# An expert layer whose items are paired by size: counts sorted on chip, biases by matmul, the first expert fetched whole, results gathered by index

## The reference

```
logits = hf @ router_w + router_b
top_logit, top_idx = lax.top_k(logits, 4)
gates = jax.nn.softmax(top_logit, axis=-1)
...
def expert_block(xb, e):
    gu = xb @ w_gu[e] + b_gu[e]                 # 1024 -> 2 x 1024
    gate, up = gu[..., :1024], gu[..., 1024:]
    gate = jnp.minimum(gate, 7.0)
    up = jnp.clip(up, -7.0, 7.0)
    y = (up + 1.0) * (gate * jax.nn.sigmoid(1.702 * gate))
    return y @ w_down[e] + b_down[e]            # 1024 -> 1024
...
out = segment_sum(y_rows * row_gate)            # four rows a token
x = x + g2 * out
result = rmsnorm(x, final_g)
```

## Time and profile before

| | |
|---|---|
| median of three runs | 3612.41 us (3611.96 to 3616.03) |
| span of the profiled execution | 3608.5 us |
| TensorE busy | 86% of the span |
| VectorE / ScalarE / GpSimd busy | 40% / 25% / 8% |
| moved by DMA | 684.11 MB, mean 190 GB/s |
| mean granted TensorE clock | 0.931 |

### The profile page before, as it was taken

How to read it: one execution, slowest core, us unless ns; L and a number is a source line. 1 busy time by engine, 2 the same in 40 slices (tenths; PEclk the granted TensorE clock), 3 DMA queues, 4 the chain that set the end, 5 groups by cost and what they waited for, 6 DMA issues and landing times. The chain is left out here.

```text
span 3608.5 us, 95079 instructions
## 1 busy us (share of the span) xinstructions
PE 3112.7 (86%) x42406; PEld 2242.3 (62%) x42406; DVE 1452.6 (40%) x2335; ACT 898.5 (25%) x1523; POOL 298.1 (8%) x236
## 2 busy tenths in 40 slices
PE   5978879998887888787897976676999999999996
PEld 3855558887565676674786866543566566666653
DVE  3355653333763554556565765524111111111111
ACT  2114322222223343332343542201011000111100
POOL 0021200000411132230000104000000000000000
PEclk7989889999898999997998987887999999999998
DMA  7242432222143101003653430222999999999993
GB/s 288 82 158 77 155 140 85 101 96 93 38 155 123 50 21 38 34 4 125 233 187 121 166 115 3 101 102 94 399 404 406 408 407 405 406 405 406 409 405 139
DMA packets 220724, 684.11 MB, mean 190 GB/s; under 512 B 26096, under 2 KB 51184, under 8 KB 187712
## 3 DMA queue, kind: packets, MB, share of 16 engines
q1 hardware_dynamic: 190288, 647.72, 46.8%
q10 hardware_dynamic: 30192, 32.77, 2.7%
HBM read 659.46 MB, written 20.97 MB: 189 GB/s over the span
## 5 line engine op out<-in xcount | busy, mean ns | idle before, releaser
L3480 PE MATMUL experts_psum_gu<-ring,experts_x 128*32 128x256 f32 x9216 | 507.9, 381 | 16.6 <-ACT experts_x L3524 16.6
L3480 PEld LDWEIGHTS experts_psum_gu<-ring,experts_x 128*32 128x32 f32 x9216 | 295.6, 110 | 219.8 <-ACT experts_x L3524 16.9
L3584 DVE TENSOR_TENSOR experts_gate<-experts_psum_gu,experts_bias 128x768 f32<-128x768 f32 x32 | 30.6, 957 | 864.4 <-PE experts_psum_gu L3480 864.4
L3503 PE MATMUL experts_psum_down<-experts_weights,experts_hiddenT 128*32 128x256 f32 x6144 | 339.0, 380 | 4.3 <-ACT experts_hiddenT L3532 4.3
L3503 PEld LDWEIGHTS experts_psum_down<-experts_weights,experts_hiddenT 128*32 128x32 f32 x6144 | 199.5, 110 | 137.9 <-issue 6.3
L818 PE MATMUL mlp_psum_bank<-mlp_x_high,mlp_w_high 128*128 128x512 f32 (+1 forms) x512 | 174.8, 341 | 12.8 <-DVE xT_rounded L322 12.8
L3528 ACT ACTIVATE experts_sigmoid<-experts_gate 128x768 f32<-128x768 f32 x32 | 27.0, 843 | 615.5 <-DVE experts_gate L3586 615.5
L296 DVE TENSOR_TENSOR ring_rounded<-ring,mlp_w_high 128x1024 fp32r<-128x1024 f32 x128 | 156.7, 1225 | 51.3 <-ACT mlp_w_high L291 51.3
L818 PE MATMUL mlp_psum_bank<-xT_rounded,mlp_w_high 128*128 128x512 f32 (+1 forms) x512 | 175.4, 342 | 0.0
L818 PE MATMUL mlp_psum_bank<-mlp_x_high,ring_rounded 128*128 128x512 f32 (+1 forms) x512 | 173.6, 339 | 0.0
L3480 PE MATMUL experts_psum_gu<-xT,experts_x 128*32 128x256 f32 x3072 | 171.6, 379 | 0.0
(11 more groups left out here) (729 smaller groups left out, 5761.9 us busy)
## 6 DMA issues: line engine op xcount, KB each, us to landing
ring<-in_w_gu SPq DMA_DIRECT2D x186, 1024.0 KB, 18.9
experts_weights<-in_w_down SPq DMA_DIRECT2D x128, 1024.0 KB, 20.7
ring<-in_ada_w SPq DMA_DIRECT2D x36, 2048.0 KB, 9.0
ring<-in_mlp_w SPq DMA_DIRECT2D x32, 2048.0 KB, 7.9
xT<-in_w_gu SPq DMA_DIRECT2D x64, 1024.0 KB, 20.3
ring<-in_w_in SPq DMA_DIRECT2D x12, 2048.0 KB, 7.6
ring<-in_ab_w_in SPq DMA_DIRECT2D x6, 2048.0 KB, 9.1
ring<-in_w_rkv SPq DMA_DIRECT2D x6, 2048.0 KB, 8.4
```

The costliest lines, as they stand in the source:

```text
L3480: mm = nc.tensor.matmul(pg[o, q, gr, :], x, w[:, c:c + C], start=(u == 0 and gr != 1), stop=(u == U - 1), skip_group_check=True)
L3503: mm = nc.tensor.matmul(pd[o, gr, :], hidT[:, ch, gr, GROUP * v:GROUP * v + GROUP], w[:, ch, C * c:C * c + C], start=(v == 0 and ch == 0 a ...
L3584: v.tensor_tensor(gt[:, :, :], pg[:, 0, 0:GROUPS, :], rep(bias[:, 0, :], GROUPS), ALU.add).then_inc(s_bg, 1)
```

## The change

- The experts are ranked by their counts on chip (`ahead`: a comparison of keys, count times 32 minus the expert's number, with expert 0 put first). Items come in pairs: an item of 96 slots from the larger half (A), an item of 64 slots from the smaller half (B). The table has expert and first slot of each; a further A item stands for an expert of more than 96 tokens. The loop goes over pairs, so its body holds an A and a B item.
- Expert 0 always comes first, and its two remaining gate/up units and four down units are loaded during the router.
- The gate/up biases are split into three bf16 parts on 96 partitions (GpSimd, during the router) and added by bf16 matmuls with a 0/1 band `who` that ScalarE copies for each item; the bias loads and VectorE's two additions go.
- A down unit holds two neighbouring rows a partition, 8 KB in one run; the hidden values are transposed with stride two to match.
- The tokens are split into two rounded parts, and the gather is rounded matmuls, four for each of 16 results.
- Results are stored by item, not by slot. At the end each (token, k) row is gathered from memory by its index (GpSimd, eight indirect DMAs of 128 rows), weighted and summed on VectorE; `gsel`, its transposes and the final matmuls go. Rows of `moe_y` that a larger count would use are set to zero in the router.

The core of the diff:

```diff
 router, sync:
     sync.dma_start(w[:, :, :], rw.rearrange("(a p) n -> p a n", p=P)).then_inc(s_ld, 16)
+    for q in range(3):
+        sync.dma_start(b32[32 * q:32 * q + 32, :, :], b_gu.rearrange("e (a n) -> e a n", a=2)).then_inc(s_b32, 16)
     sync.dma_start(bd[:, :], bdown).then_inc(s_ld, 16)
+    for u in range(GU_UNITS, UNITS):
+        sync.dma_start(unit_tile(g, base, more, u), unit_rows(w_gu, w_down, 0, u)).then_inc(s_unit[u], 16)
+    sync.wait_ge(s_l, 2)
+    sync.wait_ge(s_tok, 4)
+    for u in range(2 * SLOTS, GU_UNITS):
+        sync.dma_start(unit_tile(g, base, more, u), unit_rows(w_gu, w_down, 0, u)).then_inc(s_unit[u], 16)
+    sync.wait_ge(s_zero, 1)
+    (two stores of zeros to moe_y, 960 and 640 rows)
 router, tensor:
     for t in range(2):
-        mm = nc.tensor.matmul(pb[:, n % 4, :], htok[:, t, kt * P:(kt + 1) * P],
-                              S[:, t, sh * 512:(sh + 1) * 512], start=(t == 0), stop=(t == 1))
+        for q, x in enumerate((t_high, t_low)):
+            mm = nc.tensor.matmul(pb[:, n % 4, :], x[:, t, kt * P:(kt + 1) * P],
+                                  S[:, t, sh * 512:(sh + 1) * 512], start=(t + q == 0), stop=(t + q == 2))
 router, scalar:
+    act.wait_ge(s_split, 5)
     for n in range(2 * KT):
         act.wait_ge(s_xg, n + 1)
         nc.scalar.copy(XgT[...], pb[:, n % 4, :]).then_inc(s_xgc, 1)
 router, gpsimd:
+    for q in range(3):
+        v.tensor_copy(band[r, :, :], rep(blk(g, C_ID)[r, r], GROUP, 2)).then_inc(s_pad, 1)
+    v.memset(zero[:, :], 0.0).then_inc(s_zero, 1)
+    pool.wait_ge(s_b32, 48)
+    for rows in (96, 64, 32):
+        if rows < 96:
+            v.tensor_tensor(b32[0:rows, :, :], b32[0:rows, :, :], b96_2[0:rows, :, :], ALU.subtract).then_inc(s_split, 1)
+        v.tensor_copy(b96_2[0:rows, :, :], b32[0:rows, :, :]).then_inc(s_split, 1)
 router, vector:
+    for n in range(4):
+        v.tensor_tensor(t_low[:, n // 2, cols], pb[:, n, :], t_high[:, n // 2, cols].bitcast(F32), ALU.subtract)
-    (item table in one row; gsel: 2 x (1 + 3 x 2) operations of 1024 columns)
+    (ranks, places and table by small operations on 32 partitions; the row index yidx)

 experts, tensor:
+    for gr in range(groups):
+        for q in range(2):
+            for j in range(4):
+                c = 1024 * q + C * j
+                nc.tensor.matmul(pg[32 * j:32 * j + 32, q, gr, :], who[:, :], b96[:, c:c + C],
+                                 start=(gr != 1), stop=False, skip_group_check=True)
-    with pe.Fori(0, last) as i:
-        gate_up(i + 1)
-        down(i)
-        turn_hidden(i + 1)
+    with pe.Fori(0, last) as i:
+        gate_up(i, 1)
+        down(i, 0)
+        turn_hidden(i, 1)
+        gate_up(i + 1, 0)
+        down(i, 1)
+        turn_hidden(i + 1, 0)
 experts, scalar:
-    load_bias(expert_of(act, i + 2))
+    nc.scalar.copy(who[:, :], band[:, bass.ds(e, 1), :].rearrange("p e c -> p (e c)")).then_inc(s_who, 1)
 experts, vector:
-    v.tensor_tensor(gt[:, :, :], pg[:, 0, 0:GROUPS, :], rep(bias[:, 0, :], GROUPS), ALU.add).then_inc(s_bg, 1)
-    v.tensor_scalar(gt[:, :, :], gt[:, :, :], SWI_LIMIT, None, ALU.min).then_inc(s_gt, 1)
+    v.tensor_scalar(G, pg[:, 0, 0:groups, :], SWI_LIMIT, None, ALU.min).then_inc(s_gt, 1)

 final, gpsimd:
+    for t in range(2):
+        for k in range(TOP_K):
+            n = TOP_K * t + k
+            nc.gpsimd.indirect_dma_start(out=yl[:, n, :], out_offset=None, in_=y_dram[:, :],
+                                         in_offset=bass.IndirectOffsetOnAxis(ap=yidx[:, t, k:k + 1], axis=0))\
+                .then_inc(s_yl[n], 16)
 final, tensor:
-    (16 transposes of gsel, 64 records of matmul over the 4 MB list)
 final, vector:
+    (for each tile and k: wait for the gather; total = row * gate + total)
+    ch.link(v.tensor_tensor(total[:, t, :], total[:, t, :], gate_row, ALU.mult))
+    v.tensor_tensor(g.x[:, 2 + t, :], g.x[:, 2 + t, :], total[:, t, :], ALU.add).then_inc(s_x, 1)
```

More of the change, by code:

```diff
@@ L3194, in router @@
         mask = ph.sb("mask", [P, 2, N_EXP])
-        base = ph.sb("base", [P, 2, N_EXP])
+        start = ph.sb("slot_start", [P, 2, N_EXP])
+        rank = ph.sb("slot", [P, 2, TOP_K])
         gT = ph.sb("gatesT", [N_EXP, 2, P])
[L3197 to L3203, removed]
+        cnt = ph.sb("counts", [N_EXP, P])
+        e_col = ph.sb("expert_col", [N_EXP, 2])
+        e_row = ph.sb("expert_row", [N_EXP, N_EXP])
+        key = ph.sb("keys", [N_EXP, N_EXP + 1])
+        ahead = ph.sb("ahead", [N_EXP, N_EXP])
+        vec = ph.sb("items_counts_one", [N_EXP, 4])
+        place = ph.sb("first_start_rank", [N_EXP, 3])
+        pick = ph.sb("picked", [N_EXP, 2, N_PAIRS])
+        val = ph.sb("values", [N_EXP, 8])
+        wide = ph.sb("row_shift", [N_EXP, P])
+        shift = ph.sb("row_shift_all", [P, N_EXP])
+        yrow = ph.sb("y_row", [P, 2, TOP_K])
+        t_low = ph.sb("tokens_low", [P, 2, D], F32R)
+        zero = ph.sb("zero", [P, D])
+        t_high = g.x_rounded[:, 0:2, :]
+        b32 = XgT[0:96, 0:2, 0:1024]
         pl = ph.ps("logits", [P, 2, 512])
@@ L3244, in _ @@
                 for t in range(2):
[L3245 to L3246 removed]
+                    nc.tensor.matmul(pl[:, t, 0:N_EXP], cnt[:, :], ahead[:, :], start=True, stop=False)
                     if t:
@@ L3364, in _ @@
[L3364 to L3369 removed]
+                dve.wait_ge(s_tab, 1)
@@ L3519, in _ @@
+                gate_up(last, 1)
+                down(last, 0)
+                turn_hidden(last, 1)
+                down(last, 1)
             @block.scalar
             def _(act):
[L3521 to L3528 removed]
@@ L3570, in _, with tokens @@
-                turned(last)
-                result(last)
-                act.wait_ge(s_st, last * 64 + 128)
+                def tokens(i, kind):
+                    n = kinds[kind][0] * GROUP
+                    e = expert_of(act, i, kind)
+                    s0 = slot_of(act, i, kind)
+                    nc.scalar.copy(who[:, :], band[:, bass.ds(e, 1), :].rearrange("p e c -> p (e c)")).then_inc(s_who, 1)
+                    nc.scalar.copy(xe[:, :, 0:n], XgT[:, :, bass.ds(s0, n)]).then_inc(s_x, 1)
@@ new lines, in _ @@
+                nc.scalar.sem_inc(s_st, 64)
+                tokens(0, 0)
+                last = last_pair(act)
+                sigmoid(0, 0)
+                act.wait_ge(s_up, 1)
+                tokens(0, 1)
+                turned(0, 0)
+                with act.Fori(0, last) as i:
+                    sigmoid(i, 1)
+                    act.wait_ge(s_up, i * 2 + 2)
+                    tokens(i + 1, 0)
+                    result(i, 0)
+                    turned(i, 1)
+                    sigmoid(i + 1, 0)
+                    act.wait_ge(s_up, i * 2 + 3)
+                    tokens(i + 1, 1)
+                    result(i, 1)
+                    turned(i + 1, 0)
@@ L3573, in _ @@
+                sigmoid(last, 1)
+                result(last, 0)
+                turned(last, 1)
+                result(last, 1)
+                act.wait_ge(s_st, last * 128 + 192)
                 nc.scalar.sem_inc(s_end, 1)
@@ L3604, in final @@
+                hidden(0, 0)
+                last = last_pair(dve)
+                with dve.Fori(0, last) as i:
+                    hidden(i, 1)
+                    hidden(i + 1, 0)
+                hidden(last, 1)
+def final(g, acc, topg, yidx, yl, y_dram, gate_row, final_g, out):
     nc = g.nc
-    NS = N_PAIR // P
     with Phase(g, "final") as ph:
@@ L3898, in block2 @@
             gate_rows(g, "rows3", [lambda kt: g.mods[0][:, 40 + kt, 0:1]], rows)
-            router(g, a["router_w"], rb[:, :], iota[:, :], a["b_down"], acc, rank[:, :, :], topg[:, :, :], XgT,
-                   table, acc, gsel)
-        experts(g, a["w_gu"], a["w_down"], a["b_gu"], XgT, table, y_dram)
-        final(g, acc, gsel, y_dram, rows[:, 0, :], row(a["final_g"]), out)
+            router(g, a["router_w"], rb[:, :], iota[:, :], a["b_down"], a["b_gu"], a["w_gu"], a["w_down"], acc, S, topg, yidx,
+                   XgT, table, b96, band, more, s_unit, y_dram)
+        experts(g, a["w_gu"], a["w_down"], b96, band, more, s_unit, XgT, table, y_dram)
+        final(g, acc, topg, yidx, XgT[:, :, 0:D], y_dram, rows[:, 0, :], row(a["final_g"]), out)
 def program(nc, a, out, parts=(0, 1, 2), x_out=None):
```

482 lines of the change are left out of this document (250 added, 232 removed).

## The result

The changed kernel takes 3557.9 us (median; 3555.4 to 3562.3), the kernel before 3613.5 (3612.0 to 3616.0) beside it: a ratio of 0.9851, 95% interval 0.9837 to 0.9865. It is faster, by 56 us where 115 were forecast.

| stretch | before | after | gain | forecast |
|---|---|---|---|---|
| experts: first matmul to the final stage | 1047.5 | 1033.2 | 14.3 | 68 (72 less 4 for code) |
| start of the experts, from the span's start | 2503.8 | 2492.9 | 10.9 | 19.4 |
| final stage | 57.2 | 31.7 | 25.5 | 28 |

A forecast was written before the change was run, and what follows sets the result against it. TensorE paces the expert loop with DMA close behind, and DMA was to become its bound. 3612.4 - 72 (experts) - 19.4 (router) - 28 (final sum) + 4 (code) = 3497 us, range 3468 to 3570 us.

The forecast's parts named there:

- The step that failed: Expert loop's branch back: any wait for code (0.2 to 7.3 us a turn) mostly hides in TensorE's slack; 4 us in all.
- The code's own bytes: Expert loop: transfers of instruction code, covered together with the branch wait by one term of 4 us.
- The rival: Expert loop: branch waits 7.3 us for code, plus 3 us at low clock; pair 64.6 us, 3543 us in all; chance 0.13.
- the full queue: Expert loop: twelve weight buffers keep the DMA queue full while TensorE waits for code; an argument against that rival.
- The sign that I had named for it: Expert loop: a turn of 64 us or more with idle queues would show the forecast wrong, through code or clock.
- the likeliest case: Whole kernel: DMA-bound expert loop with the rest as summed, 3475 to 3535 us; chance 0.70.
- Experts, without the code: Expert stage: DMA becomes the bound at 420 GB/s, 400.6 MB, 61.5 us a pair, 976 us; gain 72 us before code.
- The third rival: Expert loop: clock falls while TensorE waits for DMA, the whole gain lost or up to 3735 us; chance 0.05.
- The first (406 GB/s): Expert loop: DMA stays at 406 GB/s, 33 us longer, 3530 us; counted within the 0.70 case's range.
- I count 0: Router: GpSimd's new bias work, about 30 us, stays hidden and costs 0; upper bound 17 us.
- 81.4 - 19.4 = 62.0 us: Router: gain of 19.4 us summed from bias copies, token split, faster gather, dropped selection matrices and fewer bias issues.
- Final stage: Final sum: eight gathers overlap, 15 us; VectorE ends near 20 us, stage takes 29 instead of 57.2; gain 28 us.

The follow-up runs named there:

- e2: Changed kernel with gate and up in one matmul of 512 columns, bias matmuls likewise; loop body about 1,340 matrix instructions instead of 2,020: 3500.7 us, ratio 0.9701.
- e7: Kernel before the change with gate and up in one matmul of 512 columns, all else as it was: ratio 1.0010.
- e1: Changed kernel with TensorE's experts loop written out, 15 pairs without a branch back, other engines' loops kept: 3529.2 us, ratio 0.9776.
- e4: Changed kernel with only the bias matmuls of the first two groups merged, 1,988 matrix instructions instead of 2,020: 3528.3 us, ratio 0.9769.
- e10: Changed kernel with 512-column gate/up matmuls for the items of 64 slots alone, 1,748 matrix instructions in the body: 3526.6 us.
- e14: e2 with 6 of the 8 gate/up units of an item of 96 split into 256-column matmuls again, 1,628 matrix instructions: 3498.8 us.
- e11: e2 without the load of the fourth down unit from the second item on, same matmuls: 3438.8 us.
- e9: e2 with GpSimd's five bias operations left out, biases zero: first expert 61.7 us after the router's first VectorE operation; whole time not given.

## Why the prediction was wrong

**The step that failed** is "TensorE has 7.2 us of slack a pair, so this alone mostly hides; I put 4 us for it and for the code's own bytes". The measured term is 57 us: the experts' stage takes 976.4 us where the code is kept (e2) and 1033.2 where it is not (e7 leaves nothing of that to the wider matmul). It was too small in two places.

*The code's own bytes.* In e1 TensorE shows no wait for code, and its stage is still 21 us longer than e2's. Kernels with the change's transfers move 416 to 418 GB/s in the loop where code comes in and TensorE does not hold them up (e1, e4, e10; 2 MB of it), and 422 where next to none does (e2, e14). This goes with the code in each of them; that the code is the cause was not tried by itself.

*What follows the wait.* The wait itself was bounded well (6.2 us; I had 0.2 to 7.3), and "mostly hides" held for it: e4 and e10 have it and little else, and their stages are 3 to 6 us longer than e1's. What I left out is the half clock, which only a rival had, and a second wait, which none had. 4.4 + 1.6 us of waits and 3.6 us lost to the clock (in the turn shown 7.2 us of matmuls ran at half speed) are 9.6 us a turn. TensorE's own work is 54.8 us a turn (e11) against the 60.3 us of e2's turn, so the slack is 5.5 us; 54.8 + 9.6 = 64.4. TensorE sets the pace, the units are taken later, and the queue runs empty. Of the 57 us this is the larger part, 36 us beyond e1.

The rival had it: "a pair 64.6 us", measured 64.67. That it agrees so closely is luck, since it had 7.3 us of wait and 3 of clock on 54.3. It got 0.13 because I set the slack and the full queue against the wait and not against the wait with its half clock. The sign that I had named for it came, a turn of 64 us or more with idle queues. That 3557.9 us lie inside 3468 to 3570 is no merit of the likeliest case, whose own range ended at 3535.

**Did a row tell?** The earlier trace rows said only that 1,164 instructions stay. No row of before had a longer loop to compare, so the case should have stood near even. The Trainium skill (Runtime: NRT & Kernel Launch, Instruction fetch mechanics) gives TensorE room for 2,048 instructions; the runs here put the edge for a loop's body lower, between 1,628 and 1,748 matrix instructions, with the waits and register operations on top. Its sentence on the two pages in use is not borne out: 1,628 instructions came back in 0.2 us.

**Experts, without the code: right.** e2 has each part of it: TensorE no longer the bound, 422 GB/s for my 420, 400.6 MB, a pair in 60.3 us for 61.5, 976.4 us for 976. The third rival (the clock falls as TensorE waits for transfers) did not come: 1.00 throughout with gaps of 0.6 us. The first (406 GB/s) neither. Loads landed 26.1 us after issue in e2, for the 28 forecast.

**Router: "I count 0" failed.** The prediction's 81.4 - 19.4 = 62.0 us is what e9 takes without GpSimd's five operations (61.7); with them it is 67.7. I asked when GpSimd's work ends (2445.9, earlier than my 2454) and not what it does to VectorE beside it. The rest of the shortfall is the router's later start (2.8 us), which no edit made: it is chance, within the 2418.9 to 2431.5 us given above. The Trainium skill (SBUF — State Buffer, SBUF: two separate sides) says that GpSimd and VectorE share one pair of ports as a lock, and that, of two operations that need the pair, the loser stands still until the other's instruction ends; the 2.47 us above agree, and so does the copy from PSUM that went on.

**Final stage: right.** 31.7 us for 29, gathers landing in 6 us beside each other; VectorE's sums end 22.3 us after the stage's start, for the 20 forecast.

With the measured terms in their places: 3497, less 4 for the code, plus 57.2 (1033.2 for 976), 5.7 (67.7 for 62.0), 2.8 and 2.7 (31.7 for 29), and less 3.8, since the median lies 0.1 us above the profiled span here and not 3.9: 3557.6 us, against 3557.9. This is an account, which has to come out, and no test.

## What to carry to other kernels

Count the instructions of a hardware loop's body on each engine before it is lengthened, two items to a turn or more operations in it; here TensorE's branch back went from 0.2 to 6 us between 1,628 and 1,748, and at 2,020 the long code cost 57 us: some 21 of them in the transfers (e1 pays them without any branch), the rest with the waits and the half clock behind them. Wider matmuls are a way to shorten such a body without touching its work: 3500.7 us instead of 3557.9 here. An idle engine's work isn't free because it ends in time; look at which operations of the neighbour run beside it, and with what operands.

## What was not expected of the hardware

- Written-out code (e1) had no branch and a clock of 1.00, yet its experts' stage took 21 us more than e2's. Its transfers ran at 418 GB/s instead of 422, 1.9 MB of them code, between 2540 and 3440 us; for the weights and results that is 416 instead of 421, some 12 us. Most of the rest lies at the last loads: from 3456 to 3468 us the DMA share is 0.51, at some 210 GB/s, with loads still under way. e4 and e10 show the same half share there, e2 and e14 do not. Why is open.
- A turn with long code can wait twice (4.4 and 1.6 us), and 32 instructions fewer took most of the second wait away (6.2 us are left of 22.4), not the first.
